# Repeated products of a constant matrix on TensorE between the out projection and the gather

## What is computed

```python
mixed = jnp.concatenate([y_ret, y_att], axis=-1) @ w_out[l]
x = x + gate_m * rmsnorm(mixed, g_post_mix[l])

h = rmsnorm(x, g_pre_ffn[l]) * (1.0 + scale_f) + shift_f
affinity = jax.nn.softmax((h @ w_router).astype(jnp.float32), axis=-1)
gates, idx = lax.top_k(jnp.swapaxes(affinity, 1, 2), cap)      # cap = 32, 16 experts
xe = h[b_idx, flat_idx].reshape(B, E, cap, D)
a = jnp.einsum('becd,edf->becf', xe, w_gate)                   # w_gate: 16 x 1024 x 2048
u = jnp.einsum('becd,edf->becf', xe, w_up)
ye = jnp.einsum('becf,efd->becd', jax.nn.silu(a) * u, w_down)
```

## Time and profile before

| | us |
|---|---|
| median of 3 runs | 2391.83 |
| lowest and highest | 2389.42, 2397.37 |
| span of the profiled execution (first to last instruction) | 2394.3 |

### The profile page before, as it was taken

How to read it: one execution, slowest core, us unless ns; L and a number is a source line. 1 busy time by engine, 2 the same in 40 slices (tenths; PEclk the granted TensorE clock), 3 DMA queues, 4 the chain that set the end, 5 groups by cost and what they waited for, 6 DMA issues and landing times.

```text
span 2394.3 us, 35421 instructions
## 1 busy us (share of the span) xinstructions
PE 2083.8 (87%) x15013; PEld 1643.3 (69%) x15014; DVE 825.7 (34%) x917; ACT 738.0 (31%) x804; POOL 35.5 (1%) x27
## 2 busy tenths in 40 slices
PE   7988877777777776777699999999999999999999
PEld 5858423333333322333499999999999999999998
DVE  4552100000000000000255466764454546676444
ACT  3452100000000000000244347444334334844433
POOL 0000000000000000000000002000000000200000
PEclk7997777888888888878799999999999999999999
DMA  8765699999999999999845654445564565444554
GB/s 302 269 223 228 252 429 429 429 429 428 427 429 429 429 429 428 428 428 429 320 149 165 191 175 176 160 175 184 149 215 152 164 193 170 176 164 171 180 153 126
DMA packets 235215, 657.38 MB, mean 275 GB/s; under 512 B 6933, under 2 KB 121941, under 8 KB 210517
## 3 DMA queue, kind: packets, MB, share of 16 engines
q1 hardware_dynamic: 235092, 655.62, 71.4%
HBM read 654.54 MB, written 1.05 MB: 274 GB/s over the span
## 4 chain that ended last, share of the span: by engine, by line
issue 85%; PE 14%; POOL 1%; DVE 0%; ACT 0%; POOLq 0%; DVEq 0%; ACTq 0%
PE psum L1106 4%; PE psum L1107 4%; PE psum L1108 4%; POOL work L699 0%; PE psum L1050 0%; POOL work L700 0%; POOL work L698 0%; PE psum L1130 0%; PE psum L1129 0%; PE psum L1128 0%; DVE h L2088 0%; PE psum L1061 0%; PE psum L1173 0%; ACT ring_r L1403 0%; POOL work L701 0%
## 5 line engine op out<-in xcount | busy, mean ns | idle before, releaser
L1106 PE MATMUL psum<-work_r,ring_r 128*128 128x256 f32 x2912 | 824.5, 283 | 0.1
L1108 PE MATMUL psum<-work_r,ring_r 128*128 128x256 f32 x2912 | 823.4, 283 | 0.0
L1868 DVE TENSOR_TENSOR ring_r<-ring,ring_r 128x2048 fp32r<-128x2048 f32 (+2 forms) x182 | 450.0, 2505 | 334.8 <-ACT ring_r L1403 334.8
L1106 PEld LDWEIGHTS psum<-work_r,ring_r 128*128 128x128 f32 x2912 | 558.2, 192 | 0.6 <-DVE work_r L2053 0.5
L1108 PEld LDWEIGHTS psum<-work_r,ring_r 128*128 128x128 f32 x2912 | 558.1, 192 | 0.0
L1107 PE MATMUL psum<-h_lo,ring_r 128*128 128x256 f32 x1856 | 525.2, 283 | 0.0
L1403 ACT CAST ring_r<-ring 128x2048 fp32r<-128x2048 f32 (+2 forms) x182 | 363.7, 2040 | 325.6 <-PE psum L1108 324.8
L1107 PEld LDWEIGHTS psum<-h_lo,ring_r 128*128 128x128 f32 x1856 | 356.3, 192 | 0.1
L1107 PE MATMUL psum<-work_r,ring_r 128*128 128x256 f32 x1056 | 298.6, 283 | 0.0
L1002 PE MATMUL psum<-ring,work 128*32 128x512 f32 x1536 | 216.0, 718 | 42.9 <-DMA ring<-in_w_up_e_dram 41.0
L1024 PE MATMUL psum<-ring,work 128*32 128x512 f32 x768 | 125.9, 790 | 88.6 <-DMA ring<-in_w_down_e_dram 88.5
(11 more groups left out here) (272 smaller groups left out, 1955.6 us busy)
## 6 DMA issues: line engine op xcount, KB each, us to landing
ring<-in_w_gate_e_dram SPq DMA_DIRECT2D x64, 2048.0 KB, 12.4
ring<-in_w_down_e_dram SPq DMA_DIRECT2D x48, 2048.0 KB, 31.7
ring<-in_ffn_w_up_dram SPq DMA_DIRECT2D x41, 2048.0 KB, 7.8
ring<-in_w_up_e_dram SPq DMA_DIRECT2D x32, 2048.0 KB, 21.4
work<-in_w_up_e_dram SPq DMA_DIRECT2D x32, 2048.0 KB, 30.2
ring<-in_w_in_dram SPq DMA_DIRECT2D x26, 2048.0 KB, 7.9
ring<-in_ffn_w_down_dram SPq DMA_DIRECT2D x32, 1408.0 KB, 7.1
work<-in_w_down_e_dram SPq DMA_DIRECT2D x16, 2048.0 KB, 37.5
```

The costliest lines, as they stand in the source:

```text
L1106: pe.matmul(out_b, w_hi[:, k, cols], hi[:, tokens], start=(k == 0), stop=False)
L1108: mm = pe.matmul(out_b, w_lo[:, k, cols], hi[:, tokens], start=False, stop=(k == n_k - 1))
L1868: dve.tensor_tensor(lo_unit(name, unit), raw_unit(name, unit), hi_unit(name, unit).bitcast(F32), ALU.subtract).then_inc(lo_ready, 1)
```

## The change

A float32r tile `warm_r` of 128x128 is filled once with the identity by VectorE, at the start of its program. A function `stay_warm(n)` on TensorE multiplies it by itself n times into the first 128 columns of bank 7. Nothing reads what it writes. There are 153 such products: 40 behind the first spread of the stretch, 14 behind the second, 3 behind each of the first seven chunks of the router, 60 behind `tokens_out(1)`, and 18 behind the index product. TensorE waits once for the tile, behind the out projection. An unused semaphore (`mix_ready`) goes away for the new one. Twelve blank lines at the head of the file are gone as well, which shifts the line numbers.

```diff
+        warm_r = sb("warm_r", [P, P], F32R)
-        mix_ready = sem("mix_ready")
+        warm_ready = sem("warm_ready")
@@ block.tensor, after the out projection
+            def stay_warm(n):
+
+                for _ in range(n):
+                    pe.matmul(bank[7][:, 0:P], warm_r[:], warm_r[:], start=True, stop=True)
+
+            pe.wait_ge(warm_ready, 1)
             square_sums(sq_ready, 5, 5, ms_done)
             spread_columns(rstd_ready, 2, bank[5], TT, rstd_spread)
+            stay_warm(40)
             square_sums(sq_ready, 9, 5, ms_done)
             spread_columns(rstd_ready, 3, bank[5], TT, rstd_spread)
+            stay_warm(14)
...
                     mm = pe.matmul(bank[4 + 2 * t][:, 0:E], h[:, k, P * t:P * (t + 1)], w_router[:, k, :],
                                    start=(k == 0), stop=(k == KD - 1))
+                if k + 1 < KD:
+                    stay_warm(3)
...
             tokens_out(1)
+            stay_warm(60)
 
             pe.wait_ge(spread_ready, 1)
             pe.matmul(bank[6], ones_e, spread.rearrange("p e c -> p (e c)"), start=True, stop=True).then_inc(index_done, 1)
 
+            stay_warm(18)
             pe.wait_ge(onehot_ready, 1)
@@ block.vector, at its start
             step(dve.tensor_reduce(first_rows, ident[:, 0::32], AX.X, ALU.add))
+            dve.tensor_copy(warm_r[:], ident[:]).then_inc(warm_ready, 1)
             dve.wait_ge(colsT_done, 1)
```

## The result

The changed kernel takes 2410.40 us, the median of 6 runs (2405.32 to 2414.73); the kernel before, run beside it, takes 2394.24 us (6 runs, 2389.42 to 2399.66). The ratio is 1.0067 with an interval of 1.0048 to 1.0086. So the change makes the kernel 12 to 16 us slower. The forecast was 2412.5 with a range of 2396 to 2421, built as 20.7 us on top of the 2391.8 that three runs of the kernel before had shown; beside the changed kernel it took 2394.24, 2.4 us more. Direction and total came out, but the sum behind the total did not come out in all its terms, and the rest of this document is about that.

What follows compares the result with a forecast made beforehand. The chain from out projection to gather was taken to hold up the tenth weight load; added products there cost +5.0, +1.5, +4.5, +7.5 and +2.2, together +20.7 us on 2391.8, giving 2412.5 us, range 2396 to 2421.

Steps and rivals of the forecast that it cites:

- What bounds the kernel: Chain from out projection to gather delays the tenth weight load microsecond for microsecond; TensorE time inside the full expert stream is free.
- The price of a pair: Each added weight load and matmul costs 214 ns at half clock, 113 at full, set by the float32r load.
- The terms of blocks 40, 14 and of the router: Products ahead of the second square sum, ahead of the router and inside it, at half clock: +5.0, +1.5, +4.5 us.
- The transposes are the nearest row, so I expect 0.50 throughout: Half-filled pairs, like the earlier transposes, don't raise the clock; it stays at 1.2 GHz through all added blocks.
- The terms of blocks 60 and 18: Products ahead of the index product and ahead of the clearing, all at half clock: +7.5 and +2.2 us.
- Nothing takes it back: The whole +20.7 us reaches the total, since the weight stream waits for the slot.
- Rival 1: Each added product runs in two passes, 428 ns at half clock: +16 to +28 us, 2408 to 2420; chance 0.14.
- Rival 2: The clock rises in the added blocks though the weight load binds: 2391 to 2404 us; chance 0.08.
- main case: All added products run at half clock, 214 ns each: 2412.5 us, own range 2408 to 2417; chance 0.62.
- Rivals 3 and 4: Products cheap, 107 ns at half clock: clock rises, 2385 to 2390 us, chance 0.09; or stays down, 2396, chance 0.07.

Runs made afterwards that it cites:

- inexperts: Changed kernel with its five blocks removed and 60 of the same products in every expert, between gate and up products; 2409.36 us (kernel before 2391.9).
- cols32: Changed kernel with 32 moving columns instead of 128 in each added product, same weight load; 2405.38 us (kernel before 2391.9).
- bf16: Changed kernel with the constant tile in bfloat16 instead of float32r, still 128 columns; 2394.83 us, ratio 1.0004 to the kernel before.
- after_long: Changed kernel without any edit, measured again with more executions; 2405.12 us (8 runs), ratio 1.0051 to the kernel before.
- only40: Changed kernel with only the 40 products between first spread and second square sum left; 2402.85 us (kernel before 2393.09).
- only60: Changed kernel with only the 60 products between the transposes and the index product left; 2396.83 us (kernel before 2393.09).
- before_again: Kernel before without any edit, profiled a second time; 2392.05 us.
- fit512: Changed kernel with bfloat16 products of 512 columns, counts cut to 8, 3, none in the router, 11 and 4; 2394.41 us, ratio 1.0005 to the kernel before.
- wide256: Changed kernel with 256 moving columns instead of 128 in each added product, same counts; 2397.22 us, ratio 1.0017 to the kernel before.

## Why the prediction was right, and where it was wrong

**What bounds the kernel: right.** The tenth load moved with the stretch, and the span with it: the stretch grew by 11.84 us and the span by 13.5. `inexperts` shows the other side, 60 us of added TensorE time under a DMA share of 1.01 for nothing, with one exception that the prediction hadn't made, the first expert.

**The price of a pair: right, 214 ns.** The 40 start 215.70 us and the square sum 224.28, which is 8.58/40 = 214.5. `cols32` shows that it isn't the columns, `bf16` that a type with a cheaper load takes the penalty away. At full clock, in `after_long`, it is (254.58 - 247.75)/60 = 114 ns, where I took 113. The Trainium skill ("TensorE: Matmul & The Clock Gate", section "Back-to-back issue gap") has the 81 ns for a pair that the prediction set aside. No float32r block comes to it, at 214 and 114 ns; the bf16 pairs lie on either side of it, at 107 ns at half clock and under 60 at full.

**The terms of blocks 40, 14 and of the router: right**, +4.87, +1.38 and +4.45 against +5.0, +1.5 and +4.5. `only40` gives +4.80 for the first by itself.

**"The transposes are the nearest row, so I expect 0.50 throughout": wrong.** This is the step that failed. I had read from the earlier trace rows that TensorE was busy with transposes for 4 us and the clock stayed at half, and concluded that a block of half-filled pairs wouldn't raise it either. For a block by itself that is right: the 40 stayed at half clock in all four profiles with 128 float32r columns (8.77 or 8.78 us each time). But behind the transposes the clock did rise, in `only60` with no other block, and in `only40` even with TensorE idle. The reading of the earlier trace rows ended at 240.40 with the transposes, and of what followed I only saw idle time. What decides it the runs don't settle. `only40`, `before_again`, `inexperts` and the kernel before have the same instructions from the second spread to the gather, and of the four the clock rose in `only40` alone. The Trainium skill ("TensorE: Matmul & The Clock Gate", section "Part 4: PE-mode transpose") says that transposes don't bring the full clock. The trace agrees in the last three of these, where it stayed at 0.50, and not in eight other profiles, where it rose under float32 transposes or within 1.1 us behind them (three of the changed kernel, `only40`, `only60`, `cols32`, `bf16` and `fit512`). So for these transposes that sentence can't be relied on, nor its opposite.

**The terms of blocks 60 and 18: mis-sized for that reason.** +2.01 instead of +7.5 and -0.52 instead of +2.2, together 8.2 us of the 8.9 by which the sum for the stretch was too high. Block 60 took 7.56 us, of which 1.4 at half clock, where 12.8 stood in the sum; block 18 took 2.23 where 3.85 stood, and the clearing and the steps up to the tenth load gained a little.

**"Nothing takes it back": nearly right.** The stretch from the tenth load to the last gives back 1.7 us. Of this 0.9 lies in the first expert's 96 matmuls on the first weight tiles, which find the full clock sooner (11.93 us instead of 12.87); for the rest I have no row. The tail and the layers take 3.5. The last two are what brings the total nearer to my 20.7 than the stretch is, and they are luck for the forecast: I had no term for either. So is the base: the kernel before took 2.4 us more beside the changed one than in the three runs on which the forecast stands. By differences the forecast was +20.7, and measured are +16.2 in the first measurement and +11.6 in the second. Whether the longer tail and layers are a consequence of the change stays open. The tail and the slow square sum came in all six profiles of the changed kernel and its 256-column forms (46.2 to 46.4 us, and 6.99 us or close to it for the sum), but also in `fit512` and `inexperts`, and neither in `cols32` nor, for the tail, in `bf16`. In `only60` the tail is the longest of all, 47.6 us, and the sum takes 3.99. So they don't go with the blocks as such; what they do go with isn't shown.

**The rivals.** Rival 1 (two passes) falls with the 214 ns. Rival 2 had the right idea for block 60 and the wrong one for block 40: the clock rises though the load binds, but in the changed kernel only behind the transposes, and its +1.5 for block 60 is nearer to the measured +2.01 than my +7.5. What happened lies between it and the main case. Rivals 3 and 4 hung on a cheap load, which `bf16` had and the change didn't: there the stretch came to -0.5 us.

## What to carry to other kernels

A filler product has a price, and it is set by the dearer of its weight load and its columns: here a float32r tile (214 ns a product at half clock) made 153 products cost 12 us in the stretch. In bf16 the same products cost nothing on balance, since the clock rose too, and 256 columns for the same load brought the clock back. Size each filler block from its measured price against the hole that it is to fill, at the clock of that hole, and watch the step behind it. And before any of it, work out what a full clock could give on that path; here it was 6.6 us of 2392, of which the best version kept 5 in the stretch and none that the total could show.

## What the runs showed of the hardware that wasn't expected

- A busy TensorE isn't enough to bring the clock up or hold it. In 8.77 us of back-to-back pairs of float32r with 128 columns it stayed at 1.2 GHz, and inside a block with 32 columns it fell from 2.4 to 1.2 GHz (at 247.3 us in `cols32`). It rose 5.3 us into a block of pairs of 256 columns (`wide256`), and 0.9 us behind a block of bf16 pairs of 128 (`bf16`). Once it was up, float32r pairs of 128 columns held it: in `inexperts` the first expert's 60 take 6.80 us at 1.00.
- The clock can rise while TensorE does nothing: from 245.10 to 248.50 us in `only40`, behind transposes, and then fall unused.
- The clock doesn't matter for the gather. It takes 7.61 us with the clock at 0.50 in the kernel before and at 0.78 in the mean in the changed one (the row below, 1.00 for the first 4.3 us), and the 32 gathers of the two profiles all take 7.60 to 7.62 us at means from 0.50 to 0.88.

```profile
261.31:268.92 7.61, 7.61 (x34) 7.61 (x34) 0.00 (x0) 0.00 (x0) 0.00 (x0) 0.78 0.01 2
```

- The same program can find the full clock in a part of the mixer or not (0.56 and 0.89 in the same 30 us of two executions of the kernel before), and the start of the stretch differs by 6 us between them.
